# Squares added up by GpSimd in both output projections, with another order of VectorE and ScalarE in the units behind them

## The reference

```
h = h + 0.5 * swiglu(rmsnorm(h, ffn1_norm[l]), ffn1_w_gate_up[l], ffn1_w_down[l])
u = rmsnorm(h, mix_norm[l])
main, q_mem = ...              # layer 0: chunked gated DeltaNet; layer 1: forgetting attention
h = h + concat(main, memory_attention(q_mem, ...)) @ w_out[l]
h = h + 0.5 * swiglu(rmsnorm(h, ffn2_norm[l]), ffn2_w_gate_up[l], ffn2_w_down[l])
```

## Time and profile before

| | us |
|---|---|
| median of 3 runs | 1906.71 (1905.96 to 1906.74) |
| profiled execution | 1906.48 |
| its span | 1904.1 |

### The profile page before, as it was taken

One profiled execution on the slowest core, in us unless ns is written; L12 is line 12 of the kernel. 1 busy time (PEld: TensorE's weight loads), 2 busy tenths in 40 slices (PEclk: granted clock), 3 DMA queues, 4 the chain that ended last, 5 costly groups with the idle time before them and its releaser, 6 DMA issues.

```text
span 1904.1 us, 32334 instructions
## 1 busy us (share of the span) xinstructions
PE 1892.9 (99%) x12505; PEld 1691.7 (89%) x12505; DVE 1422.0 (75%) x1646; ACT 837.2 (44%) x1130; POOL 506.7 (27%) x401
## 2 busy tenths in 40 slices
PE   9999999999999999999999999999999999999998
PEld 7889998888877899998888999998888789999887
DVE  6669994478966899998446899996446599999623
ACT  5434452245445544445224444444235564444423
POOL 1224421102914044432010344331011015444100
PEclk9999999999999999999999999999999999999999
DMA  6333333344221233333334433323351133333321
GB/s 201 110 111 95 105 89 101 91 135 138 89 75 45 69 109 110 103 95 96 102 95 144 122 110 92 107 82 116 97 202 45 45 89 110 100 99 99 123 99 67
DMA packets 313985, 195.78 MB, mean 103 GB/s; under 512 B 18543, under 2 KB 304896, under 8 KB 313394
## 3 DMA queue, kind: packets, MB, share of 16 engines
q1 hardware_dynamic: 309872, 181.76, 33.0%
q10 hardware_dynamic: 3138, 9.79, 1.5%
q0 software_dynamic: 896, 3.16, 0.5%
HBM read 188.23 MB, written 6.46 MB: 102 GB/s over the span
## 4 chain that ended last, share of the span: by engine, by line
PE 86%; DVE 6%; POOL 3%; DMA 2%; ACT 1%; issue 1%; SPq 0%; ACTq 0%; DVEq 0%; POOLq 0%
PE ps L734 27%; PE ps L736 27%; PE ps L735 27%; POOL tri L3575 1%; POOL tri_tmp L3573 1%; DMA raw<-in_ffn_w_gate_up 1%; DVE w_lo L2398 1%; DVE k L3066 1%; PE ps L1545 1%; PE ps L1573 1%; DVE w_lo L2506 1%; DVE hid_lo L2741 0%; PE ps L983 0%; PE ps L973 0%; ACT w_hi L1648 0%
## 5 line engine op out<-in xcount | busy, mean ns | idle before, releaser
L734 PE MATMUL ps<-x_hi,w_hi 128*128 128x256 f32 (+1 forms) x1774 | 568.2, 320 | 1.8 <-DVE w_lo L2506 1.6
L736 PE MATMUL ps<-x_hi,w_lo 128*128 128x256 f32 (+1 forms) x1774 | 560.1, 316 | 0.0
L735 PE MATMUL ps<-x_lo,w_hi 128*128 128x256 f32 (+1 forms) x1774 | 560.0, 316 | 0.0
L734 PEld LDWEIGHTS ps<-x_hi,w_hi 128*128 128x128 f32 x1774 | 338.3, 191 | 28.1 <-issue 5.3
L736 PEld LDWEIGHTS ps<-x_hi,w_lo 128*128 128x128 f32 x1774 | 338.2, 191 | 21.8
L735 PEld LDWEIGHTS ps<-x_lo,w_hi 128*128 128x128 f32 x1774 | 338.4, 191 | 19.8 <-issue 0.7
L2398 DVE TENSOR_TENSOR w_lo<-raw,w_hi 128x2048 fp32r<-128x2048 f32 (+1 forms) x99 | 213.7, 2159 | 145.8 <-ACT w_hi L1648 145.8
L1648 ACT ACTIVATE w_hi<-raw 128x2048 fp32r<-128x2048 f32 (+2 forms) x100 | 163.9, 1639 | 337.6 <-PE ps L736 337.0
L1718 ACT ACTIVATE w_hi<-sums 128x1024 fp32r<-128x1024 f32 (+1 forms) x153 | 161.3, 1054 | 255.4 <-PE ps L736 127.6
L734 PE MATMUL ps<-t_x,w_hi 128*128 128x256 f32 x912 | 258.9, 284 | 0.0
L3481 POOL TENSOR_TENSOR hid<-gate_up 128x512 f32 (+1 forms) x88 | 158.8, 1805 | 375.6 <-DVE sums L2501 212.9
(11 more groups left out here) (396 smaller groups left out, 2908.5 us busy)
## 6 DMA issues: line engine op xcount, KB each, us to landing
raw<-in_ffn_w_gate_up SPq DMA_DIRECT2D x174, 512.0 KB, 5.0
raw<-in_ffn_w_down SPq DMA_DIRECT2D x48, 384.0 KB, 4.0
raw<-in_ffn_w_down SPq DMA_DIRECT2D x48, 320.0 KB, 3.3
raw<-in_gdn_w_in SPq DMA_DIRECT2D x26, 512.0 KB, 4.8
raw<-in_ffn_w_down SPq DMA_DIRECT2D x20, 512.0 KB, 4.4
raw<-in_w_out SPq DMA_DIRECT2D x16, 512.0 KB, 4.5
raw<-in_kv_w SPq DMA_DIRECT2D x12, 512.0 KB, 4.4
raw<-in_mem_w_kv SPq DMA_DIRECT2D x8, 512.0 KB, 4.1
```

What stands on the lines that cost most here:

```text
L734: nc.tensor.matmul(dst, hi, xh, start=first, stop=False)
L735: nc.tensor.matmul(dst, hi, xl, start=False, stop=False)
L736: return nc.tensor.matmul(dst, lo, xh, start=False, stop=last)
```

## The change

- The squares of wout0 and wout1 are added up by GpSimd, in the two-operand add that it has for the down stages. VectorE's `add_square` goes. GpSimd's `first_sum` for unit 1 stands between the adds of squares 3 and 4.
- The direct rounding and cut of unit 1 and its second sum move from the start of up1 and up3 into the last pair of wout: on ScalarE between the squares and t_hi (`whole_lead`), on VectorE between t_three and t_lo.
- On TensorE unit 1 is B11, B21, spread, T4, where it was B11, spread, T4, B21.
- On VectorE and ScalarE the order in units 0 to 2 is another (`step`): the direct cut of unit 2 comes ahead of its second sum, unit 0's gate is scaled in step 1 and not in step 2, and ScalarE applies silu of unit 0 before it takes the first product of unit 2.
- GpSimd waits for the second sum of unit 2 before its third sum.
- In wout1 ScalarE takes the root of a one-element column, which loads that table.

```diff
@@ seven_unit
                 seven_product(to[1], direct_at(u, 0), operands("B11")).then_inc(product_done, 1)
                 if spread:
+                    seven_product(to[2], direct_at(u, 2), operands("B21"))
                     spread_sum(fed_by[name], bank=bank_of(g) + 5)
                     pe.wait_ge(t_ready, PAIRS * (x + 1))
-                seven_product(to[4], direct_at(u, 1), operands("T4"))
-                seven_product(to[2], direct_at(u, 2), operands("B21")).then_inc(product_done, 1)
+                    seven_product(to[4], direct_at(u, 1), operands("T4")).then_inc(product_done, 1)
...
@@ scalar
+            def whole_lead(name):
+                u, done = first_unit[name], DONE * units_before(name)
+                act.wait_ge(raw_in[slot(u + 1)], weights_landed(u + 1))
+                act.wait_ge(product_done, done + 1)
+                direct_round(u, 1, slice(0, PAIRS - 1)).then_inc(direct_hi, 2)
+                act.wait_ge(product_done, done + 2)
+                direct_round(u, 1, slice(PAIRS - 1, PAIRS)).then_inc(direct_hi, 1)
...
@@ scalar, step of up1 and up3
+                        if n == 0 and normed:
+                            first_sums(1, None)
+                            return
                         if n == 1 and normed:
+                            take_first(1, 1)
                             root_mean_square(fed_by[name], rstd[:], bank=bank_of(g) + 5)
+                            next_direct(1)
                             take_whole()
+                            first_sums(2, at + 4)
+                            return
                         if n == 2 and normed:
+                            silu(0, 0)
                             take_first(2, 0)
                             next_direct(2)
-                            silu(0, 0)
+                            silu(1, 1)
                             first_sums(3, at + 4)
-                            silu(1, 1)
                             return
...
@@ scalar, wout0 and wout1
                             square(name, c % 2, c, h[:, c, :])
+                        if n == PAIRS - 1:
+                            whole_lead(feeds[name])
                         t_hi(name, n)
...
@@ scalar, wout1 alone
+                    nc.scalar.activation(small[:, 5:6], ones[:, 0:1], ACT.Sqrt)
                     memory_hi(1)
...
@@ vector, feed_pair
                 t_four_three()
-                add_square(name, 2 * kk)
+                if kk == PAIRS - 1:
+                    fed = feeds[name]
+                    u = first_unit[fed]
+                    dve.wait_ge(direct_hi, sums_made(fed) + 2)
+                    direct_cut(u, 1, slice(0, PAIRS - 1))
+                    dve.wait_ge(direct_hi, sums_made(fed) + 3)
+                    direct_cut(u, 1, slice(PAIRS - 1, PAIRS)).then_inc(direct_lo, 2)
+                    second_sum(fed, u, 1, by=3)
                 t_lo()
...
@@ vector, step of up1 and up3
                         if n == 1 and normed:
                             reciprocal_of_rms(fed_by[name], rstd[:])
+                            next_direct(1)
+                            second_sum(name, u, 2)
+                            gate_scale(0, 0)
+                            first_sums(2)
+                            partial_sums(1, 1)
+                            up_second(1, 1)
+                            return
                         if n == 2 and normed:
-                            gate_scale(0, 0)
+                            gate_scale(1, 1)
...
@@ vector, wout0 and wout1
-                        if n:
-                            add_square(name, 2 * n - 1)
                         feed_pair(name, n)
...
@@ gpsimd
-                        if n == 0 and whole_first(name):
-                            after_second(1)
+                        if n < 2 and whole_first(name):
+                            after_second(n + 1)
                         third_sum(u, n + 1, i)
...
                 elif kind == "wout":
                     clear_sum(name)
-                    pool.wait_ge(evac, first_group[name] + 1)
-                    first_sum(u + KT // 2, 1, None, by=3)
+                    for c in range(KT):
+                        if c == KT - 4:
+                            pool.wait_ge(evac, first_group[name] + 1)
+                            first_sum(u + KT // 2, 1, None, by=3)
+                        add_square(name, c % 2, c)
```

More of the change, by code:

```diff
@@ L1864, in silu @@
                     def silu(n, j, i=0):
-                        steps = 3 if n == 0 and normed else 0
-                        act.wait_ge(gate_step, 4 * (before + n + 1) + steps + 8 * i)
+                        act.wait_ge(gate_step, 4 * (before + n + 1) + 8 * i)
                         nc.scalar.activation(gate_up[:, j, 0, :], gate_up[:, j, 0, :],
@@ L1915, in next_direct @@
                             act.wait_ge(product_done, done + 1)
-                            direct_round(u, 1, slice(0, PAIRS - 1)).then_inc(direct_hi, 2 if normed else 1)
+                            direct_round(u, 1, slice(0, PAIRS - 1)).then_inc(direct_hi, 1)
                             act.wait_ge(product_done, done + 2)
@@ L1944, in step @@
                         next_direct(n, i)
-                        if n == 0 and not normed:
+                        if n == 0:
                             take_first(0, 0, closed=3)
                         first_sums(n + 1, at + 4, i)
-                        if n == 1 and not normed:
+                        if n == 1:
                             silu(0, 0)
@@ L2469, in pair_columns @@
                 return t_one, t_two, t_four_three, odd_lo, even_lo, t_lo, late_lo
[L2471 to L2477, removed]
-                    dve.wait_ge(sum_ready, done)
-                nc.vector.tensor_tensor(square_sum[:], square_sum[:], gate_up[:, c % 2, 0, :],
-                                        ALU.add).then_inc(sum_ready, 1)
-            def feed_pair(name, kk):
-                t_one, t_two, t_four_three, odd_lo, even_lo, t_lo, late_lo = pair_columns(name, kk)
-                t_one()
-                odd_lo()
-                late_lo()
-                even_lo()
-                t_two()
-                t_four_three()
-                add_square(name, 2 * kk)
-                t_lo()
             def second_sum(name, u, m, i=0, by=1):
@@ L2508, in direct_cut, with feed_pair @@
                                                direct(w_hi, slot(u))[:, pairs].bitcast(F32), ALU.subtract)
+            def feed_pair(name, kk):
+                t_one, t_two, t_four_three, odd_lo, even_lo, t_lo, late_lo = pair_columns(name, kk)
+                t_one()
+                odd_lo()
+                late_lo()
+                even_lo()
+                t_two()
+                t_four_three()
+                if kk == PAIRS - 1:
[6 more added lines that the diff above has]
+                    second_sum(fed, u, 1, by=3)
+                t_lo()
             def sum_cut(s, r0, r1, at, signal, by=1):
@@ L2688, in steps_before @@
                     def steps_before(n):
-                        return 4 * (before + n) - (1 if n == 1 and normed else 0)
+                        return 4 * (before + n)
                     def partial_sums(n, j, i=0):
@@ L2700, in partial_sums @@
                                                 two_halves(ps[:, b + 1, :]), ALU.add).then_inc(
-                                                    gate_step, 4 if n == 1 and normed else 1)
+                                                    gate_step, 1)
                         dve.wait_ge(gate_step, steps_before(n) + 1 + 8 * i)
@@ L2724, in gate_scale @@
                         nc.vector.tensor_tensor(gate_up[:, j, 0, :], gate_up[:, j, 0, :], rstd[:],
-                                                ALU.mult).then_inc(gate_step, 1)
+                                                ALU.mult).then_inc(gate_step, 4 if n == 0 and normed else 1)
                     def last_sums(n, i=0):
@@ L2784, in step @@
                             next_direct(n, i)
-                        if n == 2 and normed:
-                            gate_scale(1, 1)
                         if n == 1 and not normed:
@@ L2822, in _ @@
                         if normed:
[L2823 removed]
+                            first_sums(1)
                         else:
```

16 lines of the change are left out of this document (5 added, 11 removed).

## The result

The changed kernel takes 1914.02 us (median of 6 runs, 1913.19 to 1914.66) against 1906.55 before (6 runs beside it): ratio 1.0037, 95% interval 1.0027 to 1.0048. It is slower by 7.5 us, 0.4%; 8.8 had been forecast (1915.3). The profiled spans differ by the same 7.5 (1911.6 and 1904.1).

A forecast was written before the change was run, and what follows sets the result against it. The prediction took TensorE, busy 99% of the span, as the bound, with VectorE delayed by GpSimd on their shared port. It summed +5.5 (wout1 and up3) and +3.3 (wout0 and up1) to +8.8 on 1906.5: 1915.3 us, range 1909 to 1919.5.

The forecast's parts named there:

- The case it called likeliest: Both GpSimd adds block VectorE at t_two and L2442 in each of eight pairs: 1915.3 us, chance 78%.
- Price of a pair: In wout0 and wout1, GpSimd's two adds of squares delay VectorE's t_two and L2442: 2.0 us lost per pair.
- Rival (b): In the pairs of wout0 and wout1, only one GpSimd add blocks VectorE: +2.9, 1909.4 us, chance 8%.
- (c): In the pairs, each block lasts the whole GpSimd add, 1.34 instead of 1.16: +11.6, 1918.1 us, chance 5%.
- What comes back: On VectorE in each pair, removing the odd square's add before t_one returns 0.6 us, the even one's nothing.
- Lateness at pair 3 of wout1: VectorE is 5.9 us late when pair 3 of wout1 begins, from the blocks of pairs 0 to 2.
- a block by the first sum: In pair 1, GpSimd's first sum queues behind two adds and meets VectorE's t_three: 1.1 us.
- TensorE in up3: TensorE stands 4.4 us for even_lo, partly earlier for cuts of w_out; unit 1 starts 5.9 late; up3 +5.5.
- where about 2 was given as a sign: TensorE would wait about 2 us for the direct cut ahead of unit 1, in up1 and up3.
- The new order: In units 0 to 2, old waits go; new ones come at unit 2's last cut, 1.1, and unit 3's direct cut, 0.7.
- up1, the term that was mis-sized: wout0 and up1: VectorE 3.9 late at pair 3, unit 1 2.1 late, -0.6 and +1.8 from the order: +3.3 us.
- the three waits of 0.45, 0.79 and 0.80: VectorE's waits in wout0 before pair 2's evacuation, a cut and pair 3, taken off its lateness there.

The follow-up runs named there:

- first projection only: The changed kernel's new order with GpSimd's adds of squares in wout0 alone, those of wout1 on VectorE: 1907.82 us, ratio 1.0010.
- adds only: The kernel before, with only the sixteen adds of squares of both output projections moved to GpSimd: 1916.88 us, ratio 1.0055.
- late adds: The changed kernel, with GpSimd's adds of pairs 0 to 2 waiting until VectorE's reads of the pair are done: 1907.64 us, ratio 1.0009.
- first sum later: The changed kernel, with GpSimd's first sum for unit 1 in wout1 waiting for t_lo of pair 1: 1913.62 us, ratio 1.0043.
- adds beside: The kernel before, VectorE keeping its adds, with sixteen more GpSimd adds of ones into a tile not read then: 1915.73 us, ratio 1.0050.

## Why the prediction was right

The case it called likeliest happened, by the mechanism it named. Step by step:

- **Price of a pair.** 2.0 forecast; t_two and t_four are 1.04 and 0.91 longer in wout0's groups, 1.95 together. Rival (b), one block in a pair, is out, and so is the price of (c), the whole 1.34 of an add for each block: the two adds need 2.58 behind even_lo, and VectorE loses 0.63 less. That an add holds VectorE off until it ends, which (c) took for its ground, fits these times.
- **What comes back.** 0.6 for the odd add and nothing for the even one: the idle time before t_lo rose from 0.31 to 0.91, which is the removed add's 0.60.
- **Lateness at pair 3 of wout1.** 5.9 forecast, 32.55 - 27.06 = 5.5 measured, with a block by the first sum, 1.07 for 1.1. It met t_lo (2.03 for 0.96) and not t_three as forecast, since its weights landed 1.45 after the adds had ended; a little later and it would have met the evacuation, as in wout0. So this part of the hit is luck.
- **TensorE in up3.** It stood for even_lo as forecast: 2.61 ahead of columns 6 and 7, 0.57 and 0.52 earlier for cuts of w_out, 3.7 in all for 4.4. Ahead of unit 1 it stood only 1.08, where about 2 was given as a sign: the products before it ran slower and filled 1.0 of that (last section). Unit 1 came at 1566.23, less the 2.38 by which wout1 began late: +5.4, for +5.9.
- **The new order.** The waits for the spread's sum and unit 2's direct cut are gone, and the load at the root has moved into wout1. From the second sum to the end of unit 2's last cut VectorE takes 19.4, as forecast. The new waits came where forecast, at unit 2's last cut (0.95 idle, and the slow first product behind it) and ahead of unit 3: 2.0 in each projection for 1.8.
- **up1, the term that was mis-sized.** +3.3 forecast, +1.8 measured. Lateness at pair 3 was 32.27 - 29.92 = 2.35 for 3.9, and unit 1 was 0.45 late for 2.1, with 0.29 idle ahead of it where about 2 was given as a sign. The forecast let the first sum block 1.1 in this projection as well; its weights landed later and it fell beside an evacuation. With the block, in the run of the first projection only, the lateness is 33.13 - 29.92 = 3.2. Of the 0.7 still missing, 0.24 is the block itself (t_lo at 1.82 lost 0.86, not 1.1), 0.15 the pairs at 1.95 and not 2.0, and 0.27 a reading of the rows: the idle printed is counted from the end of the instruction before, and without a wait the next one starts 0.08 to 0.09 ahead of that end (651.57 - 649.81 is 1.76 in wout0 of the kernel before, 0.87 without a wait in wout1, from 1548.35 to 1549.22), so the three waits of 0.45, 0.79 and 0.80 take in 0.09 more each.
- **The total, in part luck.** The traces add up to 1.8 + 5.1 + 0.6, the last one a longer wait for a transfer ahead of wout0 (L1229, 0.9 for 0.2). It has nothing to do with the change: over the thirteen kernels the first evacuation comes between 0.42 us earlier and 0.74 later than before. In the two projections and the units behind them it is 6.9 for the 8.8 forecast.

That adds only is dearer than the change (+10.7 for +7.5) had not been forecast as such. In its trace unit 1 begins 2.5 us later than before in up1 and 7.1 in up3, where the changed kernel has 0.5 and 5.4: with the direct cut ahead of t_lo, less of VectorE's lateness reaches TensorE. Against that, the changed kernel has the new waits of 2.0 in each projection. The kernel of adds only has none of these, but loses 1.7 in up1 to a slower TensorE (last section), a term that the forecast does not have.

## What to carry to other kernels

Work given to GpSimd is paid by VectorE if GpSimd reads SBUF while VectorE runs instructions with two SBUF inputs: here an add of 0.69 us on VectorE became about 1.0 of blocking, in a place where half of the adds had cost VectorE nothing, since they lay in its wait for ScalarE. Before moving work there, look in the timeline at what VectorE does in that stretch, not at its busy share; what only wrote cost nothing here, and an evacuation from PSUM kept its 1.21 to 1.22 us beside an add. If the move is made anyway, hold the operation back with a wait until such a place: that returned 6.0 of the 7.5 us. It did not make the move pay: with the late adds the kernel was no faster than before.

## What the runs showed of the hardware that was not expected

After standing 2.45 us for even_lo, TensorE ran twelve 256-column products at full clock and then slowed. By windows of the changed kernel (stretch, its length, TensorE busy and count, granted clock, share of DMA, GB/s):

```profile
1561.30:1562.82 1.52, 1.52 (x12) 1.00 0.00 0
1562.82:1565.10 2.28, 2.28 (x8) 0.51 0.02 4
1566.20:1570.30 4.10, 4.07 (x28) 0.99 0.00 0
```

A granted clock of 0.51 is the lower of its two levels, 1.2 for 2.4 GHz. Two products before the wait, at 1558.23 and 1558.46, were 0.23 apart; those from 1562.82 on are 0.43 apart, 5 x 0.20 = 1.0 us in all. Here it was hidden, since TensorE then waited for the direct cut. The clock was at 0.50 and 0.51 in the same place of the kernels of adds only and of the first sum later, behind waits of 2.47 and 2.35, and of adds beside, behind 2.57.

In the kernel of adds only it was not hidden. These are its rows at unit 1 of up1, and then two of the kernel before, whose unit 1 starts at 662.63:

```profile
664.89 0.39 PE L734 MATMUL ps<-x_hi,w_hi 128*128 128x256 f32 x1 [2.33 <-DVE w_lo L2494]
...
667.06 1.91 PE L953 MATMUL ps<-square_sum,ones 128*128 128x512 f32 x2
...
669.24 0.28 PE L734 MATMUL ps<-t_x,w_hi 128*128 128x256 f32 x1
```

```profile
664.06 1.02 PE L953 MATMUL ps<-square_sum,ones 128*128 128x512 f32 x2
...
665.27 0.28 PE L734 MATMUL ps<-t_x,w_hi 128*128 128x256 f32 x1
```

From unit 1's first product to the same product of T4 it takes 4.35 us for 2.64, with a granted clock of 0.50 from 666.5 to 669.0 and no wait in between: 1.7 us of the 10.7 that this kernel loses. So a wait of about 2.3 us can cost more than itself. It need not: behind 2.23 at the same place of the kernel of adds beside the clock stayed at 1.00, and behind 1.49 in the kernel of late adds too. The forecast had no term for it.
